# Stick-breaking attention: the causal mask taken from TensorE's sum into DVE's running product and a POOL multiply

## The reference, cut to what matters

```python
z = jnp.einsum('bhqd,bhkd->bhqk', qb, kb) * inv_sqrt_d
mask = kpos < qpos
log_beta = jax.nn.log_sigmoid(z)
log_1m_beta = jnp.where(mask, log_beta - z, 0.0)
suffix = lax.cumsum(log_1m_beta, axis=3, reverse=True) - log_1m_beta
a = jnp.where(mask, jnp.exp(log_beta + suffix), 0.0)
outs.append(jnp.einsum('bhqk,bhkd->bhqd', a.astype(vb.dtype), vb))
```

## Time and profile before

| | |
|---|---|
| median of 3 executions | 2800.58 us (2798.49 to 2803.13) |
| profiled execution, span from first to last instruction | 2802.3 us |
| PE busy over the span | 97% |
| DVE, ACT, POOL busy | 58%, 42%, 40% |
| the attention stage, about 699 to 1104 us | 405 us: PE 385, DVE 300, POOL 229, ACT 222 |
| granted TensorE clock, mean | 0.992 |

### The profile page before, as it was taken

How to read it: one execution, slowest core, us unless ns; L and a number is a source line. 1 busy time by engine, 2 the same in 40 slices (tenths; PEclk the granted TensorE clock), 3 DMA queues, 4 the chain that set the end, 5 groups by cost and what they waited for, 6 DMA issues and landing times.

```text
span 2802.3 us, 38646 instructions
## 1 busy us (share of the span) xinstructions
PE 2707.3 (97%) x13208; PEld 2150.3 (77%) x13208; DVE 1614.1 (58%) x2120; ACT 1189.8 (42%) x1779; POOL 1109.0 (40%) x753
## 2 busy tenths in 40 slices
PE   6999999999999998999999999999999999989998
PEld 4788888787777776878886777777788888868886
DVE  7744443304676776583015555554436766788888
ACT  4211123323555555442236667765434433334442
POOL 1222222121555554212221111211123988858886
PEclk9999999999999999999999999999999999999999
DMA  5333321344211213113330101101443343374442
GB/s 228 128 127 120 120 98 45 103 146 140 76 54 45 82 52 114 59 38 111 121 108 31 38 32 37 38 30 61 150 158 120 128 161 141 136 259 158 159 161 92
DMA packets 102110, 294.74 MB, mean 105 GB/s; under 512 B 9856, under 2 KB 10496, under 8 KB 101504
## 3 DMA queue, kind: packets, MB, share of 16 engines
q1 hardware_dynamic: 102016, 293.56, 29.7%
HBM read 220.12 MB, written 73.40 MB: 105 GB/s over the span
## 4 chain that ended last, share of the span: by engine, by line
PE 60%; issue 25%; POOL 6%; DVE 4%; ACT 3%; DMA 1%; POOLq 0%; SPq 0%; ACTq 0%; DVEq 0%
PE PS L847 27%; PE PS L1331 10%; PE PS L1383 5%; PE PS L1077 5%; POOL WL L2747 3%; PE PS L1049 2%; PE PS L982 2%; PE PS L1011 2%; PE PS L1026 2%; PE PS L1235 2%; POOL dL L2860 1%; PE PS L1216 1%; DVE dM L2679 1%; DVE bC L2296 1%; PE PS L1175 1%
## 5 line engine op out<-in xcount | busy, mean ns | idle before, releaser
L2747 POOL TENSOR_TENSOR WL<-WR,WH 128x1024 fp32r<-128x1024 f32 x147 | 367.7, 2501 | 1359.9 <-ACT WH L1421 1252.6
L847 PE MATMUL PS<-HH,WH 128*128 128x512 f32 x1712 | 546.0, 400 | 19.4 <-POOL WL L2747 5.9
L847 PE MATMUL PS<-HL,WH 128*128 128x512 f32 x1712 | 531.6, 392 | 0.0
L847 PE MATMUL PS<-HH,WL 128*128 128x512 f32 x1712 | 530.0, 391 | 0.0
L847 PEld LDWEIGHTS PS<-HH,WH 128*128 128x128 f32 x1712 | 315.4, 189 | 95.9 <-issue 26.3
L847 PEld LDWEIGHTS PS<-HL,WH 128*128 128x128 f32 x1712 | 323.4, 189 | 69.3
L847 PEld LDWEIGHTS PS<-HH,WL 128*128 128x128 f32 x1712 | 323.2, 189 | 69.3
L1421 ACT ACTIVATE WH<-WR 128x1024 fp32r<-128x1024 f32 x147 | 155.6, 1059 | 324.1 <-PE PS L847 226.6
L2771 POOL TENSOR_TENSOR bB<-bB,bC 128x256 f32<-128x256 f32 (+7 forms) x128 | 191.2, 1504 | 191.1 <-DVE bC L2296 191.1
L2296 DVE TENSOR_TENSOR_SCAN bC<-bN,EPSC 128x256 f32<-128x256 f32 (+7 forms) x128 | 222.7, 1751 | 57.3 <-ACT bN L1607 52.4
L2679 DVE TENSOR_TENSOR dM<-PS,dM 128x512 f32<-128x512 f32 x212 | 136.2, 678 | 1.6 <-PE PS L1383 1.2
(11 more groups left out here) (348 smaller groups left out, 5618.7 us busy)
## 6 DMA issues: line engine op xcount, KB each, us to landing
WR<-wst SPq DMA_DIRECT2D x149, 512.0 KB, 3.4
uRAW<-wst SPq DMA_DIRECT2D x32, 512.0 KB, 4.8
hid<-uT SPq DMA_DIRECT2D x32, 512.0 KB, 2.8
dRAW<-wst SPq DMA_DIRECT2D x64, 256.0 KB, 3.6
HLF<-hid SPq DMA_DIRECT2D x28, 512.0 KB, 8.9
GLF<-hid SPq DMA_DIRECT2D x28, 512.0 KB, 8.1
TMP<-mods SPq DMA_DIRECT2D x24, 512.0 KB, 4.2
MR<-mods SPq DMA_DIRECT2D x24, 512.0 KB, 5.3
```

The costliest lines, as they stand in the source:

```text
L847: last = pe.matmul(PS[:, dst0 + q:dst0 + q + HALF], l, rr[:, k * S + q:k * S + q + HALF], start=a, stop=z)
L2747: pool.tensor_tensor(WL[slot][:, :], WR0[:, :], WH[slot][:, :].bitcast(F32), ALU.subtract).then_inc(w_lo, 1)
```

## The change

The four mask matmuls of every `scores(t)` and their operands go, and the last score matmul of each head raises `b_s`. The running product reads a mask tile bM as its second operand, with `max` in place of `bypass`: bM is 0 before the diagonal block and in that block 1 where k >= q, so the product stays at 1 there. POOL multiplies the diagonal block of bB by BELOW (1 where k < q, 0 elsewhere) before it waits for the product, in an instruction of 128 columns of its own, and waits for its end (`b_m`) before the multiply by the product. DVE makes bM and BELOW once, before the first round. Since bM needs 4 KB per partition, one of the four staging tiles of `STG["y"]` moves onto the place of the first query tile.

```diff
-        IDR = place("IDR", P, F32R)
-        TRIR = place("TRIR", P, F32R)
-        IDRS = place("IDRS", P, F32R)
-        TRIRS = place("TRIRS", P, F32R)
+        BELOW = place("BELOW", P)
...
+        bM = place("bM", S, F32, r)
...
-               for name, at, places in (("y", (B_KV + 127) // 128 * 128, (0, 2, 4, 6)), ("ab", slots, (0, 2, 4, 6)))}
+               for name, at, places in (("y", (B_KV + 127) // 128 * 128, (0, 2, 4)), ("ab", slots, (0, 2, 4, 6)))}
+        STG["y"].append(nc.alloc_sbuf_tensor_at("STGy3", [P, S], F32, offset=slots))
...
PE, scores(t)
-                                pe.matmul(PS[:, base + c0:base + c0 + w], l[par][rows, q], rr[par][rows, c0:c0 + w],
-                                          start=i == 0, stop=i == 2 and c0 + w < n)
-                    for ident, tri in ((IDR, TRIR), (IDRS, TRIRS)):
-                        for h in range(2):
-                            rows, base = slice(h * HD, (h + 1) * HD), (1 + h) * S
-                            last = pe.matmul(PS[:, base + t * P:base + (t + 1) * P], ident[rows, :], tri[rows, :],
-                                             start=False, stop=ident is IDRS)
-                            if ident is IDRS:
-                                last.then_inc(b_s, 1)
+                                last = pe.matmul(PS[:, base + c0:base + c0 + w], l[par][rows, q], rr[par][rows, c0:c0 + w],
+                                                 start=i == 0, stop=i == 2)
+                                if i == 2 and c0 + w == n:
+                                    last.then_inc(b_s, 1)
ACT, once
-            act.wait_ge(ld_c, 48)
-            act.activation(IDR[:, :], IDF[:, :], ACT.Identity)
-            act.activation(TRIR[:, :], TRF[:, :], ACT.Identity)
-            for h in range(2):
-                rows, other = slice(h * HD, (h + 1) * HD), slice((1 - h) * HD, (2 - h) * HD)
-                act.activation(IDRS[rows, :], IDF[other, :], ACT.Identity)
-                act.activation(TRIRS[rows, :], TRF[other, :], ACT.Identity)
DVE, once, before the first round
+            links(dve.memset(bM[:, 0:S - P], 0.0))
+            links(dve.tensor_scalar(bM[:, S - P:S], TRF[:, :], -1.0 / BIG, None, ALU.mult))
+            dve.tensor_scalar(BELOW[:, :], TRF[:, :], 1.0 / BIG, 1.0, ALU.mult, ALU.add).then_inc(b_m, 1)
+            dve.wait_ge(b_m, 1)
DVE, left(t, h)
-                    dve.tensor_tensor_scan(bC[h][:, S - n:S][:, ::-1], c, EPSC[:, 0:1].broadcast_to([P, n]), 1.0,
-                                           ALU.mult, ALU.bypass).then_inc(b_l[h], 1)
+                    dve.tensor_tensor_scan(bC[h][:, S - n:S][:, ::-1], c, bM[:, S - n:S][:, ::-1], 1.0,
+                                           ALU.mult, ALU.max).then_inc(b_l[h], 1)
POOL, attention_b
                 if first:
                     pool.wait_ge(free[1], u[1])
+                    pool.wait_ge(b_m, 1)
                 for t in range(ST):
                     n = (t + 1) * P
                     for h in range(2):
                         pool.wait_ge(free[1 + h], ST * j + (u[1 + h] + t + 1))
+                        diag = bB[t % 2][h][:, t * P:n]
+                        pool.tensor_tensor(diag, diag, BELOW[:, :], ALU.mult).then_inc(b_m, 1)
+                        pool.wait_ge(b_m, 2 * ST * j + (2 * t + h + 2))
                         pool.wait_ge(b_l[h], ST * j + (t + 1))
                         b = bB[t % 2][h][:, 0:n]
                         pool.tensor_tensor(b, b, bC[h][:, S - n + 1:S + 1], ALU.mult).then_inc(b_a, 1)
```

More of the change, by code:

```diff
@@ L470, in block_kernel @@
         b_a = sem("b_a")
+        b_m = sem("b_m")
         b_t = sem("b_t")
@@ L1017, in scores @@
                     q = slice(t * P, (t + 1) * P)
-                    diag = slice(t * P, (t + 1) * P)
                     for h in range(2):
```

## The result

The changed kernel takes 2809.13 us in the median of six runs (2808.42 to 2810.78), the kernel before 2799.53 in six (2798.01 to 2803.13): ratio 1.0033, 95% interval 1.0023 to 1.0043. It is slower by some 9.6 us. That lies inside the stated range, 8 us above the predicted 2801, and close to the rival "POOL's multiply becomes the bound" with its 2810; the forecast's own range, 2795 to 2807, is missed.

What follows compares the result with a forecast made beforehand. PE sets the pace, but DVE and POOL, sharing SBUF access, fill t = 5 to 7. Terms +0.6 - 0.7 + 0.6 = +0.5 on 2802.3 give 2802.8, median forecast 2801; own range 2795 to 2807, stated range 2788 to 2811.

Steps and rivals of the forecast that it cites:

- POOL's multiply becomes the bound: Rival: PE waits at t = 6's transposes for the second multiply, behind four masks at 0.41 + 0.28 each; 2810, chance 0.22.
- the slower side: Outcome for the whole kernel: slower than before by over 0.2% (5.6 us), chance 0.28.
- What bounds the kernel: Attention stage: PE sets the pace, but at t = 5 to 7 DVE and POOL are full, 25.2 of 26 us.
- The port: DVE's running products and POOL instructions reading SBUF treated as one resource: the later stands still, saving only some 0.15 us.
- Price of a mask matmul: PE's four mask matmuls per block cost 0.23 us at t = 0 and 4, 0.17 at the others; 11.8 in all.
- The shift at t = 5: PE's saving before t = 5, 0.97 us plus some 0.2 from the earlier signal, starts that block's products 1.2 earlier.
- the walk: Instruction-by-instruction timing of t = 5 to 7 in a middle round: about +0.1 us a round, +0.6 for six.
- The running product: DVE's product with max and a real tile costs the same 1.76 and 2.02 us for 768 and 896 columns.
- A POOL mask: POOL's 128-column mask: 0.41 us undisturbed, 0.26 after release if held up, plus some 0.1 waiting for its own end.
- Who goes first: When a DVE product and a POOL instruction both wait, the one that had waited longer goes first.
- First round: PE's order differs and DVE and POOL are less crowded, so half of PE's saving stays: -0.7 us.
- Last round: Closing transposes wait for POOL's multiply behind two masks and two waits, about 0.9, less 0.3 for earlier start: +0.6 us.

Runs made afterwards that it cites:

- the masks of 8 columns: The changed kernel with POOL's mask multiply narrowed from 128 to 8 columns, semaphores and waits kept: 2797.42 us, ratio 0.9988 to the kernel before.

## Why the prediction was right or wrong

The time lies in the stated range, but on the slower side, which had 0.28 against 0.46 for no change; the sum was +0.5, and the stage shows +10.4: +4.15 in the middle rounds (forecast +0.6), +3.4 in the first (-0.7) and +2.9 in the last (+0.6). The order of events at t = 5 to 7 was foreseen; the sum went wrong at PE's shift, at the first and last rounds, and at the clock, for which it had no term. By its own steps:

- **What bounds the kernel: right.** The port is what t = 5 to 7 wait for, and the masks of these blocks alone carry the middle rounds' loss (51.67 with those of t = 5 and 6 only).
- **Price of a mask matmul: right, its worth was not.** At t = 6 the group without masks takes 984.22 to 984.71, 0.49, as the earlier trace rows had it. But I let all eight blocks save, 1.48 us. At t = 0, 3 and 7 PE stands, soon behind the scores, at the eviction of the projection's bank, and only the other five blocks give anything: 0.8. The masks filled a wait that the profile could not show as one. The scores of t = 1 to 7, counted from the round's first score matmul, start 0.01, 0.17, 0.34, 0.34, 0.55, 0.72 and 0.88 us sooner than before (sixth round of both): t = 0 and 3 give nothing, the others 0.16 to 0.21 each. That the whole edit came to 9.3 us all the same, near the forecast's 11.8, is partly luck: the first and last rounds gave 4.5 to 5.2 where 3.0 were forecast, partly by the clock.
- **The shift at t = 5: the step that failed in the middle rounds.** It should have been 1.2 us, of which t = 0 and 3 were to give 0.40 and gave none. In the kernel before, the first bN of that block starts 26.69 us after the round's first score matmul, in the changed one 25.97 (952.45 to 978.42): 0.72. With it everything in the walk comes 0.35 to 0.5 later, as the traces have it: first product 979.26 where the walk says 978.8, bQL starts at 992.35 and the walk has 992.0, the second multiply of t = 6 ends at 998.73 and the walk says 998.3. So a middle round changes by +0.69, not +0.1: 4.15 in place of 0.6. The shift explains some 0.45 of the 0.6 between the two; the rest is not accounted for one by one.
- **The running product: right.** 1.76 us for 768 columns where nothing is in its way.
- **A POOL mask: right within 10%.** 0.45 undisturbed instead of 0.41, and the wait for its own end 0.08 to 0.16. The rival that came nearest in time had priced the wait at 0.28, which is wrong; it had the place right. Its 2810 is luck: it put 7.8 us on the six middle rounds, which took 4.15, 1 on the last and nothing on the first, which took 2.9 and 3.4.
- **Who goes first: right** in every case of the walk.
- **First round: wrong in sign.** I left it half of PE's saving, -0.7, and it lost 3.4. Without POOL's masks it is 2.3 shorter, so between no masks and all of them there are 5.7, and the clock goes from 1.00 to 0.93 between the two (at most 3.5 of the 5.7, by the estimate above). In this round PE has no step at all between the scores and the first transposes at any t (the first column of B_FIRST is 0 throughout), and the masks lie on the path at short blocks as well. An example is t = 2, where a mask stood behind the second product, which stood behind split_w. The fence has the changed kernel's POOL, then its PE; PE's wait for the multiply was 1.71 before and is 2.93 now. Right behind it the granted clock fell to the lower level (0.50 from 707 to 710), and the projection's steps started 0.43 us apart instead of 0.23.

```profile
704.14 1.11 POOL L2762 TENSOR_TENSOR bB<-bB,BELOW 128x128 f32<-128x128 f32 x1
705.32 0.86 POOL L2766 TENSOR_TENSOR bB<-bB,bC 128x384 f32<-128x384 f32 x1
...
706.24 0.55 PE L1011 MATMUL PS<-IDF,bB 128*128 128x128 f32 x3 [2.93 <-POOL bB L2766]
```

- **Last round: too small.** +0.6 forecast, +2.9 measured (+3.6 against the second profile of the kernel before). The closing mask at 1102.85 took 1.43 us, and PE's wait for POOL in front of the last transposes is 2.38 instead of 1.84. I had counted only these closing masks; with those of the blocks before it is longer, too, 3.5 us at t = 0 to 4 (63.18 against 59.67) and 1.0 at t = 5 and 6 (60.65), with the clock at 0.95 and 0.94 against 0.97.
- **The clock: no term in the sum.** It falls in the first and last rounds of nearly every profile, and for longer with POOL's masks (0.93 and 0.92). That is at most 3.7 of the 10.4 us. How much of it the masks cause, by making PE wait, and how much is chance is not shown: before one of the falls PE had waited 2.93 us for a mask's block, but two kernels that did the same up to there differed in it.

The Trainium skill, "SBUF — State Buffer", section "Who interferes with whom", has the order of issue decide which of the two engines blocks the other. The traces here agree in kind (a mask of 0.45 us that stood behind a product took 2.17), and the masks of 8 columns show the consequence: a short instruction pays for the long one in front of it.

What stays open: how the cost in the first and the last round splits between the masks and the clock, and over the blocks. With masks at t = 0 to 4 the first round is 3.4 longer, with those at t = 5 and 6 it is 2.6 longer, of which 1.6 came before any mask.

## What to carry to other kernels

Before moving work from a busy engine to one that looks half idle, lay the timelines of all engines that share a resource side by side and add up their work in the crowded stretch, not over the stage; here 25 of 26 us were taken while POOL showed 229 us of 405. Work on the busiest engine may be free: if it stands in front of a wait for a bank or buffer, the wait is invisible as long as the work fills it. To find out, measure the distance between the two ends of that dependency, not the recorded wait. And before a stretch is compared between two profiles, look at the granted clock of both: here it made one stretch of 33 matmuls last 5.95 us instead of 4.36.

## What the runs showed of the hardware

A running product with max and a real second tile costs the same as mult with bypass and a broadcast column (1.76 us for 768 columns in both, where nothing is in its way). Between a DVE product and a POOL multiply that both want to go, the one that had waited longer went first, also when DVE's next product was issued back to back (986.42, split_w before the product that ended at 992.4). A POOL instruction that waits for its predecessor's semaphore starts 0.08 to 0.16 us after that one's end. With TensorE's granted clock at its lower level (0.50), the projection's matmuls of 512 columns started 0.43 us apart instead of 0.23, and of two kernels that had run alike up to that point one kept 1.00 and the other fell.
